# Moving the weight slots of a TensorE-bound layer: pitch 4160 bytes instead of 4096

## The chip, the cores and the metric

The kernel runs on one core of one Trainium2 chip. The metric is the time of one execution in device microseconds; the median of several executions counts, and lower is better.

## What is computed

One layer of a language model on 512 rows of 1024 numbers, all in float32: a gated feed-forward block (SwiGLU), a mixer of dilated attention and an mLSTM, an attention over 256 memory rows, and a second SwiGLU, each followed by a residual and a layer norm. Nearly all of the arithmetic is products of activations with weight matrices:

```python
def reference(x, mem, rel_bias, ln_g, ln_b, ffn_w_gate, ffn_w_up, ffn_w_down, w_in, ...):
    for l in range(DEPTH):          # DEPTH = 1
        x = layer_norm(ALPHA * x + 0.5 * swiglu(x, ffn_w_gate[l, 0], ffn_w_up[l, 0], ffn_w_down[l, 0]), ...)
        x = layer_norm(ALPHA * x + hybrid_mixer(x, w_in[l], ..., w_out[l], rel_bias), ...)
        x = layer_norm(ALPHA * x + memory_attention(x, mem, xq_w[l], xkv_w[l], xo_w[l]), ...)
        x = layer_norm(ALPHA * x + 0.5 * swiglu(x, ffn_w_gate[l, 1], ffn_w_up[l, 1], ffn_w_down[l, 1]), ...)
    return x
...
def swiglu(x, w_gate, w_up, w_down):
    return (jax.nn.silu(x @ w_gate) * (x @ w_up)) @ w_down
```

Here d_model is 1024, the feed-forward width 2816 (22 tiles of 128), and the mixer's input projection is 3592 wide.

## The kernel before

**Weights come in units.** All weights are cut into 204 units of 128 partitions by 1024 float32, 512 KB each, in the order in which they are used. SyncE's queue brings a unit into one of three `raw` tiles. ScalarE copies it, rounded to the type float32r, into `whi`; VectorE writes the rest, `raw - whi`, into `wlo` (line 1234 of the profile, in the helper `split`). There are six slots of each, `whi0` to `whi5` and `wlo0` to `wlo5`, and unit u lies in slot u mod 6. Activations are split in the same way: `xth`/`xtl` for the transposed input of a stage, `hhi`/`hlo` (six slots) for what a down projection reads, `mth`/`mtl` for the memory.

**Three matmuls make a product.** The helper `three` writes lines 393 to 395 of the profile: high by high, high by low, low by high, all into the same PSUM bank. With 128 by 128 stationary and 128 by 512 moving, these are the bulk of the program: 4,440 matmuls of 512 columns, and 384 more of the same kind with 256 columns. In a name like `ps<-xth,whi` the first is the moving operand and the second the stationary one, which a weight load (PEld) brings into the array ahead of its matmul.

- In `cols_part` (feed-forward up, projections) the stationary operand is a 128-column piece of a weight slot, and the activations move.
- In `product` (all four down or output projections), in `rows_block` and in the memory's value projection the weight slot's halves of 512 columns move, and pieces of the activations (`hhi`, `xth`, `mth`) are stationary.

**Order.** Every engine has a program of its own that is written out by hand, with loops over six units in the feed-forward stages; semaphores tie them together. A slot is used for a visit of 3, 6, 12 or 24 matmuls in a row before TensorE goes to another slot: counted over the program with its loops there are 380 visits, 128 of them of 3 matmuls, 80 of 6, 16 of 12 and 156 of 24.

**Addresses.** SBUF tiles are placed by a cursor. `sb()` gives the next bytes of every partition. In bytes within a partition, the kernel before has `whi0` at 32896 and every further slot 4096 on, `wlo0` at 57472, `raw0` at 82048, `hhi0` at 108416 and `xth` at 132992. The activations' pieces that a matmul uses start at multiples of 512 bytes from their tile's start, and so do those of a slot. Hence all 128-column weight pieces and all activation pieces have one fixed distance modulo 512 bytes: (32896 - 132992) mod 512 = 256. One small product is an exception: the gate projection, 24 matmuls of 512 columns with a stationary operand of only 36 columns, reads `wg_hi` at 225216 and `wg_lo` at 226368 with a step of 144 bytes from one k to the next.

Of the kernel before, what the change touches and what calls it, by code (L numbers as in the profile page):

```python
# [7 lines left out]
F32R = mybir.dt.float32r  # L8
# [4 lines left out]
P = 128  # L13
# [4 lines left out]
SPL = 6  # L18
# [37 lines left out]
def macaron_layer(nc, x, mem_cols, ln_g, ln_b, units, gate_cols, ig_bias, fg_bias, ml_g,  # L56
                  bias_by_key, lnm, conv_cols, g_rows, out):
    S, D = x.shape[1], x.shape[2]
# [52 lines left out]
    with ctx:  # L111

        KB = 1024
# [3 lines left out]
        cursor = [start]  # L117

        def at(name, shape, offset, dt=F32):
            return nc.alloc_sbuf_tensor_at(name, shape, dt, offset=offset)  # L120

        def sb(name, shape, dt=F32):
            n = 4
            for s in shape[1:]:
                n *= s
            t = at(name, shape, cursor[0], dt)
            cursor[0] += -(-n // 32) * 32
            assert cursor[0] <= start + size, "SBUF is full"
            return t

        xn = sb("xn", [P, NB, D])
        whi = [sb(f"whi{s}", [P, D], F32R) for s in range(SPL)]
        wlo = [sb(f"wlo{s}", [P, D], F32R) for s in range(SPL)]
        raw = [sb(f"raw{s}", [P, D]) for s in range(RAW)]
        ident = sb("ident", [P, P])
        mlg = sb("mlg", [P, MW])
# [1583 lines left out]
```

## Time and profile before

| | |
|---|---|
| time, median of 3 (lowest to highest) | 1194.47 us (1193.79 to 1195.27) |
| time of the profiled execution | 1195.15 us |
| its span in the profile | 1193.3 us |
| TensorE matmuls busy | 1181.4 us, 99% of the span |
| weight loads busy (beside the matmuls) | 968.0 us, 81% |
| VectorE busy | 539.5 us, 45% |
| ScalarE busy | 407.8 us, 34% |
| granted TensorE clock, mean | 0.995 of full speed |

The span is from the first to the last instruction; 1.85 us of the execution lie around it. A busy share near 100% says that some matmul was always under way, and not how fast they follow each other: matmuls overlap, and each lasts longer than the distance to the next one's start. The distances between starts are what sets the time here, and they are read from the timeline.

### The profile page before, as it was taken

To read this page: it belongs to the slowest core of one execution; us is meant where nothing else is said; L and a number is where in the kernel's file an instruction comes from. 1 tells how busy PE (TensorE), PEld (TensorE's weight loads), DVE (VectorE), ACT (ScalarE), POOL (GpSimd) and SP (SyncE) were. 2 spreads that over 40 slices of the span, in tenths; PEclk is the share of its full clock that TensorE was granted. 3 is DMA by queue.
4 is the path that set the end of the run, shared out by engine and by line. 5 is a ranking of instruction groups with operands and counts; after the bars stand their busy time and mean duration, and the time that the engine had idled before them with its cause. 6 is when DMAs were issued, how large, how long until landed. Compare 5 with 4: busy or idle time off the path is not lost.

```text
span 1193.3 us, 14742 instructions
## 1 busy us (share of the span) xinstructions
PE 1181.4 (99%) x5522; PEld 968.0 (81%) x5522; DVE 539.5 (45%) x840; ACT 407.8 (34%) x666; POOL 30.3 (3%) x45
## 2 busy tenths in 40 slices
PE   9999999999999999999999999999999999999997
PEld 8888888888888777788798887778988888888886
DVE  4533333443346544644885843337433333343335
ACT  5321222242324344433454454434322212232322
POOL 2000000000001011000000000000000000000000
PEclk9999999999999999999989999999999999999999
DMA  8523222232222221141333261122322232232311
GB/s 293 200 94 105 88 93 101 89 124 95 99 70 89 82 69 53 56 156 63 94 136 96 99 211 53 54 78 96 127 89 95 99 104 89 90 120 97 99 35 70
DMA packets 33563, 120.85 MB, mean 101 GB/s; under 512 B 3900, under 2 KB 3916, under 8 KB 33264
## 3 DMA queue, kind: packets, MB, share of 16 engines
q1 hardware_dynamic: 30528, 109.07, 27.5%
q0 software_dynamic: 2992, 11.19, 2.6%
q8 instruction: 30, 0.49, 0.2%
q14 instruction: 13, 0.11, 0.0%
HBM read 118.13 MB, written 2.11 MB: 101 GB/s over the span
## 4 chain that ended last, share of the span: by engine, by line
PE 99%; ACT 1%; DVE 0%; issue 0%; DVEq 0%; POOL 0%; POOLq 0%; ACTq 0%
PE ps L393 30%; PE ps L395 29%; PE ps L394 29%; PE ps L592 2%; PE ps L615 2%; PE ps L815 1%; PE ps L805 1%; PE ps L693 1%; PE ps L410 1%; PE ps L602 1%; PE ps L677 1%; PE ps L544 0%; PE ps L630 0%; PE ps L787 0%; ACT ew L844 0%
## 5 line engine op out<-in xcount | busy, mean ns | idle before, releaser
L1234 DVE TENSOR_TENSOR wlo<-raw,whi 128x1024 fp32r<-128x1024 f32 x196 | 240.5, 1231 | 413.2 <-ACT whi L844 412.3
L393 PE MATMUL ps<-xth,whi 128*128 128x512 f32 (+1 forms) x924 | 359.1, 389 | 0.0
L395 PE MATMUL ps<-xth,wlo 128*128 128x512 f32 (+1 forms) x924 | 353.2, 382 | 0.0
L394 PE MATMUL ps<-xtl,whi 128*128 128x512 f32 (+1 forms) x924 | 352.9, 382 | 0.0
L844 ACT ACTIVATE whi<-raw 128x1024 fp32r<-128x1024 f32 (+1 forms) x204 | 206.9, 1037 | 153.8 <-PE ps L395 141.8
L393 PEld LDWEIGHTS ps<-xth,whi 128*128 128x128 f32 x924 | 173.8, 188 | 34.1 <-issue 1.3
L394 PEld LDWEIGHTS ps<-xtl,whi 128*128 128x128 f32 x924 | 173.9, 188 | 33.8 <-issue 1.0
L395 PEld LDWEIGHTS ps<-xth,wlo 128*128 128x128 f32 x924 | 173.7, 188 | 33.6
L393 PE MATMUL ps<-whi,hhi 128*128 128x512 f32 x480 | 189.4, 395 | 0.0
L395 PE MATMUL ps<-whi,hlo 128*128 128x512 f32 x480 | 186.9, 389 | 0.0
L394 PE MATMUL ps<-wlo,hhi 128*128 128x512 f32 x480 | 186.8, 389 | 0.0
L844 ACT ACTIVATE eg<-ps 128x512 f32<-128x512 f32 x44 | 26.3, 598 | 326.3 <-PE ps L395 326.3
L393 PEld LDWEIGHTS ps<-whi,hhi 128*128 128x128 f32 x480 | 90.1, 188 | 19.3 <-issue 0.7
L395 PEld LDWEIGHTS ps<-whi,hlo 128*128 128x128 f32 x480 | 90.1, 188 | 19.0
L394 PEld LDWEIGHTS ps<-wlo,hhi 128*128 128x128 f32 x480 | 90.1, 188 | 18.8 <-issue 0.7
L1301 DVE SCALAR_TENSOR_TENSOR h<-eg,ps 128x512 f32 (+1 forms) x44 | 30.3, 688 | 82.2 <-PE ps L395 82.0
L844 ACT ACTIVATE squares<-xn,nmean 128x1024 f32<-128x1024 f32 x16 | 18.5, 1153 | 76.2 <-DVE nmean L1264 76.2
L393 PE MATMUL ps<-whi,xth 128*128 128x512 f32 x96 | 38.0, 396 | 0.0
L395 PE MATMUL ps<-whi,xtl 128*128 128x512 f32 x96 | 37.5, 390 | 0.0
L394 PE MATMUL ps<-wlo,xth 128*128 128x512 f32 x96 | 37.4, 389 | 0.0
L1261 DVE SCALAR_TENSOR_TENSOR xn<-xn,ps 128x512 f32<-128x512 f32 x32 | 21.3, 683 | 26.2 <-PE ps L395 26.2
L844 ACT ACTIVATE lg<-lg,nmax 128x128 f32<-128x128 f32 (+3 forms) x32 | 18.0, 562 | 42.7 <-DVE nmax L1406 42.7
(156 smaller groups left out, 936.0 us busy)
## 6 DMA issues: line engine op xcount, KB each, us to landing
raw<-in_units SPq DMA_DIRECT2D x204, 512.0 KB, 3.3
gb<-in_ln_g POOLq DMA_DIRECT2D x4, 512.0 KB, 3.8
gb<-in_ln_b POOLq DMA_DIRECT2D x4, 512.0 KB, 5.1
xn<-in_x POOLq DMA_DIRECT2D x4, 512.0 KB, 12.7
wb<-in_bias_by_key POOLq DMA_DIRECT2D x8, 256.0 KB, 3.7
out<-xn SPq DMA_DIRECT2D x8, 256.0 KB, 2.1
gsp<-g_rows POOLq DMA_DIRECT2D x1, 1024.0 KB, 7.3
memn<-in_mem_cols POOLq DMA_DIRECT2D x1, 1024.0 KB, 4.9
```

Source lines behind the costliest of these rows:

```text
L393: mm(dst, lh, rh, start=start, stop=False)
L394: mm(dst, lh, rl, start=False, stop=False)
L395: return mm(dst, ll, rh, start=False, stop=stop)
L410: last = nc.tensor.transpose(ps[2 * b + k // 4][:, (k % 4) * P:(k % 4 + 1) * P], xn[:, b, k * P:(k + 1) * P], ident[:, :])
L592: mm(ps[n % 2][:, 0:(i + 1) * P], qk[(2 * p) % 4][rows, i * P:(i + 1) * P], qk[(2 * p + 1) % 4][rows, 0:(i + 1) * P], start=True, stop=Tru ...
L602: last = nc.tensor.transpose(ps[2 + n % 2][:, j * P:(j + 1) * P], lg[n % 3][:, j * P:(j + 1) * P], ident[:, :])
L615: last = mm(ps[4 + n % 2][:, 0:HD], pt[n % PTS][:, j * P:(j + 1) * P], va[:, j, h * HD:(h + 1) * HD], start=j == 0, stop=j == i)
L677: mm(ps[j % 2][:, 0:S - j * P], qk[(2 * h + 1) % 4][:, j * P:(j + 1) * P], qk[(2 * h) % 4][:, j * P:S], start=True, stop=True).then_inc(kq ...
L844: return nc.scalar.activation(*a, **k)
L1234: v.tensor_tensor(wlo[c % SPL][:, :], raw[c % RAW][:, :], whi[c % SPL][:, :].bitcast(F32), ALU.subtract).then_inc(lo_done, 1)
L1261: step.inc(v.scalar_tensor_tensor(out=half, in0=half, scalar=ALPHA, in1=ps[2 * b + h][:, :], op0=ALU.mult, op1=ALU.add, accum_out=xsum[:, ...
L1301: v.scalar_tensor_tensor(out=dst, in0=e[:, :], scalar=0.25, in1=ps[bank + 1][:, :], op0=ALU.mult, op1=ALU.mult).then_inc(h_done, 1)
```

## The change

The cursor no longer gives the slots one after another. They are put at addresses of their own, 4160 bytes apart (4096 + 64). The first `whi` slot lies 256 bytes behind the cursor, and the `wlo` slots 25088 bytes behind the `whi` slot of the same number, a multiple of 512. Everything that is allocated later moves up by 1152 bytes.

```diff
         xn = sb("xn", [P, NB, D])
-        whi = [sb(f"whi{s}", [P, D], F32R) for s in range(SPL)]
-        wlo = [sb(f"wlo{s}", [P, D], F32R) for s in range(SPL)]
+        PITCH = 4 * KB + 64
+        slots = [cursor[0] + 256, cursor[0] + 256 + SPL * PITCH + 128]
+        whi = [at(f"whi{s}", [P, D], slots[0] + s * PITCH, F32R) for s in range(SPL)]
+        wlo = [at(f"wlo{s}", [P, D], slots[1] + s * PITCH, F32R) for s in range(SPL)]
+        cursor[0] = slots[1] + SPL * PITCH
         raw = [sb(f"raw{s}", [P, D]) for s in range(RAW)]
```

`whi0` is now at 33152, `whi1` at 37312, and so on; `wlo0` at 58240, `hhi0` at 109568, `xth` at 134144. The distance between slot s and the activations, modulo 512, was 256 for every slot; it is now 384 + 64 s, so 384, 448, 0, 64, 128 and 192 for slots 0 to 5. Slots 1, 3 and 5 are at 64 modulo 128 from the activations, slots 0, 2 and 4 at 0. No instruction is added, removed or moved on any engine or queue, no operand changes its size or type, and no semaphore or wait changes; behind the edit the line numbers are 3 higher.

## Rows read from the trace of the kernel before

**Rows 1.** The page: span, engines' busy time, chain that ended last.

```profile
span 1193.3 us, 14742 instructions
PE 1181.4 (99%) x5522; PEld 968.0 (81%) x5522; DVE 539.5 (45%) x840; ACT 407.8 (34%) x666; POOL 30.3 (3%) x45
...
PE 99%; ACT 1%; DVE 0%; issue 0%; DVEq 0%; POOL 0%; POOLq 0%; ACTq 0%
```

**Rows 2.** Waits: engine line waited for, total us, times, longest us.

```profile
DVE wlo L1234 <- ACT whi L844: 412.3, 113, 12.5
...
ACT whi L844 <- PE ps L395: 141.8, 46, 3.9
...
PEld ps L615 <- ACT pt L844: 9.1, 14, 0.8
...
PE ps L693 <- DVE pt L1480: 1.6, 1, 1.6
```

**Rows 3.** Timeline of TensorE: start us, duration us; three moments 100 us apart.

```profile
99.92 0.39 PE L393 MATMUL ps<-xth,whi 128*128 128x512 f32 x1
...
199.88 0.39 PE L393 MATMUL ps<-xth,whi 128*128 128x512 f32 x1
...
299.84 0.39 PE L393 MATMUL ps<-whi,hhi 128*128 128x512 f32 x1
```

**Rows 4.** Stretches, line 394 alone: length, busy (matmuls), clock, DMA, GB/s.

```profile
50.00:350.00 300.00, 171.67 (x442) 1.00 0.29 96
850.00:1180.00 330.00, 188.87 (x486) 1.00 0.27 91
```

**Rows 5.** Timeline, matmuls of 256 columns.

```profile
836.01 0.28 PE L393 MATMUL ps<-xth,whi 128*128 128x256 f32 x1
...
836.37 0.28 PE L393 MATMUL ps<-xth,whi 128*128 128x256 f32 x1
```

**Rows 6.** Timeline, plain float32 matmuls of 512 columns, and their group.

```profile
761.82 1.88 PE L815 MATMUL ps<-xpt,vmem 128*128 128x512 f32 x4
...
L815 PE MATMUL ps<-xpt,vmem 128*128 128x512 f32 x32 | 14.9, 592 | 0.0
```

**Rows 7.** Timeline into, through and out of the gate projection.

```profile
389.16 0.39 PE L393 MATMUL ps<-whi,xth 128*128 128x512 f32 x1
...
389.84 0.39 PE L393 MATMUL ps<-xth,wg_hi 128*36 128x512 f32 x1
390.07 0.39 PE L394 MATMUL ps<-xtl,wg_hi 128*36 128x512 f32 x1
390.30 0.39 PE L395 MATMUL ps<-xth,wg_lo 128*36 128x512 f32 x1
390.52 0.39 PE L393 MATMUL ps<-xth,wg_hi 128*36 128x512 f32 x1
...
392.61 0.39 PE L393 MATMUL ps<-xth,wg_hi 128*36 128x512 f32 x1
392.84 0.39 PE L394 MATMUL ps<-xtl,wg_hi 128*36 128x512 f32 x1
393.06 0.40 PE L395 MATMUL ps<-xth,wg_lo 128*36 128x512 f32 x1
...
395.38 0.40 PE L393 MATMUL ps<-xth,whi 128*128 128x512 f32 x1
```

**Rows 8.** Timeline after transposes have broken the stream.

```profile
361.01 0.39 PE L394 MATMUL ps<-wlo,hhi 128*128 128x512 f32 x1
...
361.71 0.39 PE L394 MATMUL ps<-wlo,hhi 128*128 128x512 f32 x1
361.93 0.39 PE L395 MATMUL ps<-whi,hlo 128*128 128x512 f32 x1
362.16 0.40 PE L393 MATMUL ps<-whi,hhi 128*128 128x512 f32 x1
362.40 0.39 PE L394 MATMUL ps<-wlo,hhi 128*128 128x512 f32 x1
...
363.09 0.39 PE L394 MATMUL ps<-wlo,hhi 128*128 128x512 f32 x1
```

**Rows 9.** VectorE's splits: duration ns min/median/max, first and last start.

```profile
L1234 DVE TENSOR_TENSOR wlo<-raw,whi x196: 1192/1225/2712, 22.5 to 1154.9; 128x1024 fp32r<-128x1024 f32 x196
```

## The prediction

> **What bounds the kernel now.** I read the page first. TensorE is busy for 99% of the span and makes up 99% of the chain that ended last [rows 1]. The list of waits says the same from the other side: TensorE's longest wait for another engine is 1.6 us in one matmul, and its weight loads wait for ScalarE for 9.1 us in all, inside the attention; VectorE on the other hand waits 412.3 us for ScalarE's halves of the splits, and ScalarE 141.8 us for TensorE to give slots back [rows 2]. So only a change in the distance between matmul starts can move the time much.
>
> That distance is astonishingly constant. Three starts of line 393 lie 99.96 and again 99.96 us apart [rows 3]. Line 394 has 442 matmuls in the 300 us from 50 to 350 [rows 4], so about 147 per 100 us, and with the other two lines 441 matmuls: 99.96 / 441 = 226.7 ns each. The third of these starts lies in the down projection, where the weight slot moves and `hhi` is stationary, while in the first two it is the other way round. So through every slot, through the change of role, and through all multiples of 512 bytes within the tiles, the distance stays the same. The stretch 850 to 1180 has 486 in 330 us, the same pace [rows 4]. The granted clock is 1.00 there, which is the 2.4 GHz level: 512 columns are 213.3 ns, and 13.3 ns come on top. With 256 columns three matmuls take 0.36 us [rows 5], so 120 ns each, 106.7 + 13.3: the same addition. The plain float32 matmuls don't have it: four of them last 1.88 us from first start to last end, one lasts 592 ns, so three distances are 1.29 us and one 429 ns, against 426.7 ns for 1024 array cycles [rows 6], so some 2 ns on top. The 4,440 matmuls of 512 columns are 4,440 x 226.7 ns = 1006.5 us, 84% of the span, and 11 ns in each, 49 us, are this unexplained addition. The question of the change is whether that addition depends on the distance between the addresses of the two operands.
>
> **What the change costs, part by part.** The addresses are the only thing that changes, and there are four places where they could act.
>
> (a) *The steady pace in slots 0, 2 and 4.* Their distance to the activations was 256 modulo 512 and is now 384, 0 and 128. Between 199.88 and 299.84 the moving address goes from `xth` (384 modulo 512) to `whi` (128), a move by 256, with no mark in the 226.7 ns [rows 3]. Nothing before shows a move by 128. I take 0 for these.
>
> (b) *The steady pace in slots 1, 3 and 5*, now at 64 modulo 128. The nearest rows are those of the gate projection. At its k = 0, `wg_hi` lies 64 bytes from `xth` modulo 512 (225216 - 132992) and `wg_lo` 192, both a position that the odd slots get. The matmuls start at 389.16, 389.84 and 390.52: three distances before and three after the entry are 0.68 us each, so 226.7 ns, while the stationary operand changed from distance 256 to 64 and to 192 [rows 7]. At k = 4 the distances are 128 and 256: 392.61, 392.84, 393.06 is 0.45 us for two, again the old pace [rows 7]. The same projection also shows the other bound. Its steps of 144 bytes put most k at 16, 32 or 48 modulo 64, and from 390.52 to 395.38 its 21 matmuls take 4.86 us, 231.4 ns each, 4.7 ns more [rows 7]. So positions do matter when they are off a multiple of 64. All slots are at multiples of 64 before and after. The low bound for 2,220 matmuls in the odd slots is 0, the high one 2,220 x 4.7 ns = 10.4 us. I take 0, by the rows with the same positions.
>
> (c) *The jump by 64 bytes from visit to visit.* When the stream is disturbed, it doesn't return to 226.7 ns at once: after transposes, nine distances from 361.01 to 363.09 are 2.08 us against 9 x 226.7 = 2.04, so 41 ns over [rows 8]. They alternate: 361.71 to 361.93 is 0.22, 362.16 to 362.40 is 0.24 [rows 8]. If each of the 380 visits began such a walk, its cost would be 41 ns in the 172 visits of 12 or 24 matmuls, and by the same walk, cut off at six and at three matmuls, some 29 ns in 80 visits and 18 ns in 128: 7.1 + 2.3 + 2.3 = 11.7 us. The entry to the gate projection, a jump by 192 bytes, began none [rows 7]. That gives 0 at the low end. I take 1 ns a visit, 0.4 us.
>
> (d) *The other engines.* VectorE reads `raw` and `whi` together, until now at equal positions modulo 4096, and takes 1225 ns [rows 9]; that may become somewhat less or more. It is covered: a unit lasts 24 x 226.7 ns = 5.4 us on TensorE, a split 1.2 us, and VectorE waits 412.3 us in all [rows 2]. Even 300 ns more in each of 196 splits would be 59 us in those waits. If that cover went, in the attention, what is late next is the weight load that waits for `pt`, now 9.1 us in all [rows 2]; I put it at 0. Transfers, their sizes and targets in number are the same.
>
> Sum: 0 + 0 + 0.4 + 0 us. The profiled execution took 1195.15 us (span 1193.3), 0.7 us over the median of 1194.47; I put the sum on the median: 1194.9 us.
>
> The Trainium skill, page "TensorE: Matmul & The Clock Gate", section "Part 2: What happens when you issue a matmul", says that TensorE has two independent SBUF read ports, one for the moving operand and one for weight loads, so that a load takes no bandwidth from the running matmul. By that rule no distance of addresses could matter, in either direction, and the change would be worth 0. The same section gives N / 2.4 + 2.5 ns for the distance of warm matmuls, which is 215.8 ns; the float32 rows agree with the 2.5, and the float32r rows at 226.7 do not. So the rule's arithmetic leaves 11 ns that something takes, and the gate projection shows that positions can add to them.
>
> **The rivals.**
>
> *Faster: the 11 ns are a conflict of the two read streams.* Weight load and moving stream start nearly together in every matmul, all at one distance modulo 512. If that distance is a bad one, and other multiples of 64 are better, up to 11 ns a matmul come back: at most 49 us, 1146 us. More likely only some slots gain, or all gain little: the shortest distance that the walk shows is 0.22 us [rows 8]; I take its upper end, 224 ns, 2.7 ns less, which over all 4,440 is 12 us, 1182.5 us. For it speaks that the addition exists at all, that float32 matmuls, which take their moving columns at half the rate, don't have it, and that the walk shows shorter distances. Against it: a stationary operand of 36 columns (28% of the load) paid the full addition in three matmuls, at two other distances [rows 7], and 256 columns pay as much as 512 [rows 5]. A conflict would shrink with the load. Chance 0.21.
>
> *Slower: positions at 64 modulo 128 never settle.* The mechanism is that of the gate projection's later k, 231.4 ns instead of 226.7. It would come in the odd slots, or where these move, for which there is no row at all: the moving address has never been at an odd multiple of 64 from its usual one. In the odd slots alone it gives 10.4 us, 1205 us; in all slots 20.9 us, 1215 us. It decides from 0.54 ns a matmul on, 2.4 us in all. For it: those rows. Against it: k = 0 and k = 4. Chance 0.16.
>
> *Slower: a walk at each visit*, as in (c): between 0.4 and 11.7 us, with the middle near 6, 1200 us. For it speaks the length of the walks after a break; against it the entry at 389.84 and the way from stationary `whi` to stationary `hhi` between 199.88 and 299.84, neither of which begins one. Chance 0.10.
>
> *No change*, since positions in steps of 64 bytes don't count: chance 0.53, 1193 to 1197 us by itself.
>
> **How the numbers follow.** A measurement of this kernel tells about 0.2%, 2.4 us, from no change. The walk at small cost ends within that in a third of its cases, as would the smallest of the other two: faster 0.21, same 0.55, slower 0.24. The range goes down to 1183 us, which takes in a gain of up to 2.6 ns a matmul and leaves out the larger ones, and up to 1205 us, which takes in the walks and the unsettled odd slots and leaves out unsettled slots everywhere; that leaves some 0.2 outside. The likeliest case gives 1194.9.
>
> **What the changed profile would show.** If I am right, three starts of line 396 (393 before) stay 99.96 us apart, through slots of both kinds, and busy time and matmul counts per stretch don't move. If slots differ, the distance within a unit of 24 matmuls changes with a period of six units, about 33 us, and the timeline of two neighbouring units shows it: 5.44 us for each now. A walk shows as the first 4 to 9 distances of a unit between 224 and 236 ns and the rest at 226.7. A gain by (a) shows as 215 to 224 ns in every unit. VectorE's median of 1225 ns will tell whether its two reads at equal positions cost anything; it should leave the end where it is. What would make the prediction wrong is above all the moving operand at 64 modulo 128, in 1,824 matmuls of which half are in odd slots, since no row covers it.

## The result, and the profile after

The changed kernel takes 1210.5 us (median of 4, 1210.18 to 1211.34), the kernel before 1194.82 us (median of 4): the ratio is 1.0136, with a 95% interval of 1.0124 to 1.0147. It is slower by 15.7 us, and 5.5 us beyond the upper end of the predicted range.

The page of the changed kernel, span, busy times and VectorE's splits:

```profile
span 1208.7 us, 14742 instructions
...
PE 1196.9 (99%) x5522; PEld 966.8 (80%) x5522; DVE 537.5 (44%) x840; ACT 407.6 (34%) x666; POOL 31.3 (3%) x45
...
L1237 DVE TENSOR_TENSOR wlo<-raw,whi 128x1024 fp32r<-128x1024 f32 x196 | 239.5, 1226 | 423.0 <-ACT whi L847 422.4
```

Against [rows 1] the span grew by 15.4 us and TensorE's busy time by 15.5, while VectorE and ScalarE are no busier. The number of instructions is the same. VectorE's wait for ScalarE grew from 412.3 to 422.4 us, and ScalarE's for TensorE to give slots back from 141.8 to 146.3. So nobody keeps TensorE waiting; its matmuls follow each other more slowly.

Two stretches, one inside the first up projections and one inside the first down projection; columns as in [rows 4], but all matmuls counted. First the kernel before:

```profile
60.00:240.00 180.00, 180.00 (x795) 1.00 0.29 95
256.00:346.00 90.00, 90.00 (x399) 1.00 0.28 94
```

and the changed kernel:

```profile
60.00:240.00 180.00, 180.00 (x783) 1.00 0.29 96
256.00:346.00 90.00, 90.00 (x391) 1.00 0.30 98
```

The counts include some 1.7 matmuls that began before the stretch, so the paces are about 180 / 793.3 = 226.9 ns and 180 / 781.3 = 230.4 ns, and for the down projection 90 / 397.3 = 226.5 and 90 / 389.3 = 231.2; they are good to 0.3 ns, and where a pace below differs from such a quotient, the unrounded starts decide. The granted clock is 1.00 in all four. The loss is spread over the whole stretch, and the timeline shows how. These are the starts of seven units of 24 matmuls, in slots 1, 2, 3, 4, 5, 0 and 1, and then four starts in the down projection, of slots 0, 1, 2 and 3:

```profile
56.20 0.40 PE L396 MATMUL ps<-xth,whi 128*128 128x512 f32 x1
...
61.70 0.40 PE L396 MATMUL ps<-xth,whi 128*128 128x512 f32 x1
...
67.16 0.40 PE L396 MATMUL ps<-xth,whi 128*128 128x512 f32 x1
...
72.76 0.39 PE L396 MATMUL ps<-xth,whi 128*128 128x512 f32 x1
...
78.33 0.39 PE L396 MATMUL ps<-xth,whi 128*128 128x512 f32 x1
...
83.84 0.39 PE L396 MATMUL ps<-xth,whi 128*128 128x512 f32 x1
...
89.41 0.40 PE L396 MATMUL ps<-xth,whi 128*128 128x512 f32 x1
...
283.26 0.39 PE L396 MATMUL ps<-whi,hhi 128*128 128x512 f32 x1
...
288.83 0.39 PE L396 MATMUL ps<-whi,hhi 128*128 128x512 f32 x1
...
294.42 0.39 PE L396 MATMUL ps<-whi,hhi 128*128 128x512 f32 x1
...
299.90 0.40 PE L396 MATMUL ps<-whi,hhi 128*128 128x512 f32 x1
```

The units take 5.50, 5.46, 5.60, 5.57, 5.51 and 5.57 us, where each took 5.44. Divided by 24 and read from the unrounded starts, with the stationary operand's distance from the moving one (stationary minus moving address, modulo 256 bytes; why 256 and not 512 is shown below the table and by the pairs):

| | slot 0 | 1 | 2 | 3 | 4 | 5 |
|---|---|---|---|---|---|---|
| up: distance | 128 | 192 | 0 | 64 | 128 | 192 |
| up: ns a matmul | 232.2 | 229.3 | 227.5 | 233.2 | 232.3 | 229.4 |
| down: distance | 128 | 64 | 0 | 192 | 128 | 64 |
| down: ns a matmul | 232.1 | 232.8 | 228.4 | 229.6 | 232.8 | 233.5 |

Away from the first and last units of each projection these values repeat from round to round within 0.1 ns. Slots 0 and 4 lie 256 bytes apart in their distance modulo 512 (384 and 128), and so do slots 1 and 5 (448 and 192); each pair has one pace. In the down projection the weight slot moves and `hhi` is stationary, so the sign of its distance turns, and slots 1 and 5 change places with slot 3. Only slot 2, at distance 0 modulo 256, has the later starts of each unit 226 and 227 ns apart. In the up projection its first four are 236, 228, 233 and 231, a walk of some 20 ns in all; in the down projection the first ten (228, 229, 234, 236, 224, 231, 235, 229, 232, 231) are some 42 ns over. These walks are what its means show.

Where the 15.4 us of span lie, read from the two timelines: the stream starts again after transposes at 360.70 us in the kernel before and at 368.31 in the changed one, 7.6 us later; the second feed-forward block's 512-column stream starts at 848.97 and at 858.03, so 9.1 us later; and the end is 15.4 us later. The two feed-forward parts lost 7.6 and 6.3 us, and the 490 us between them only 1.5. Two parts of these differences are not the change's. Of the 7.6 us 0.8 are the very first matmuls, of which three follow each other at 427 or 594 ns in the changed kernel and none at more than 335 ns in the kernel before. And in the memory attention, where TensorE has idled for 1.34 and 1.60 us, the granted clock of the kernel before fell to the 1.2 GHz level (0.50) and that of the changed kernel did not (1.00). The same 20 matmuls of 129 columns, and the distance to what follows, took 4.3 us before and 2.3 after. A row of the timeline and a stretch inside it (columns as above), first before, then changed:

```profile
599.37 4.67 PE L693 MATMUL ps<-vx,pt 128*128 128x129 f32 x20 [1.60 <-DVE pt L1480]
...
599.40:603.60 4.20, 4.20 (x19) 0.50 0.00 0
```

```profile
609.24 2.50 PE L696 MATMUL ps<-vx,pt 128*128 128x129 f32 x20 [1.60 <-DVE pt L1483]
...
609.30:611.40 2.10, 2.10 (x19) 1.00 0.00 0
```

With the first matmuls behind them these distances hide 2.4 us of the change's cost. The clock's fall does not follow the addresses: of the kernels below that ran at the old pace, the one with weights and activations moved together kept the clock at 1.00 there (profiled execution 1193.57 us), and the one with pairs of slots lost it for a part of this stretch (1194.6 us). So without the clock the 490 us lost 3.9 and not 1.5.

### The profile page after: what moved, and what is told of

The parts are those of the page before. It is cut to its first block, busy times and chain, and to the rows that moved or that the text cites. A ratio compares the mean times of both kernels' runs of the same rounds, so it can differ in the third digit from the quotient of the medians.

```text
span 1208.7 us, 14742 instructions
## 1 busy us (share of the span) xinstructions
PE 1196.9 (99%) x5522; PEld 966.8 (80%) x5522; DVE 537.5 (44%) x840; ACT 407.6 (34%) x666; POOL 31.3 (3%) x45
## 4 chain that ended last, share of the span: by engine, by line
PE 99%; ACT 1%; DVE 0%; issue 0%; DVEq 0%; POOL 0%; POOLq 0%; ACTq 0%
PE ps L396 30%; PE ps L398 29%; PE ps L397 29%; PE ps L595 2%; PE ps L618 2%; PE ps L818 1%; PE ps L808 1%; PE ps L413 1%; PE ps L696 1%; PE ps L605 1%; PE ps L680 1%; PE ps L547 0%; PE ps L633 0%; PE ps L790 0%; ACT ew L847 0%; PE ps L434 0%
## 5 line engine op out<-in xcount | busy, mean ns | idle before, releaser
L1237 DVE TENSOR_TENSOR wlo<-raw,whi 128x1024 fp32r<-128x1024 f32 x196 | 239.5, 1226 | 423.0 <-ACT whi L847 422.4
L847 ACT ACTIVATE whi<-raw 128x1024 fp32r<-128x1024 f32 (+1 forms) x204 | 206.7, 1036 | 158.1 <-PE ps L398 146.3
L847 ACT ACTIVATE squares<-xn,nmean 128x1024 f32<-128x1024 f32 x16 | 18.5, 1153 | 78.5 <-DVE nmean L1267 78.5
```

Of the source, the lines that this page charges most:

```text
L847: return nc.scalar.activation(*a, **k)
L1237: v.tensor_tensor(wlo[c % SPL][:, :], raw[c % RAW][:, :], whi[c % SPL][:, :].bitcast(F32), ALU.subtract).then_inc(lo_done, 1)
```

## The experiments

**Theory A**: the pace of float32r matmuls depends on the distance between stationary and moving operand modulo 256 bytes, and 0 is the cheapest. **Theory B**: what costs is the jump from slot to slot, a walk at each visit. **Theory C**: the position of the slot itself counts. The kernels below place each slot at its address in the kernel before plus an offset in bytes, given for the high and the low slots; `room` is by how much everything behind the slots moves up. Up to the gate projection's, the kernels differ from the kernel before in lines like these.

**All slots moved by 64 bytes** (pitch 4096, no jumps):

```diff
-        whi = [sb(f"whi{s}", [P, D], F32R) for s in range(SPL)]
-        wlo = [sb(f"wlo{s}", [P, D], F32R) for s in range(SPL)]
+        hi_off, lo_off, room = [64] * 6, [64] * 6, 512
+        whi = [at(f"whi{s}", [P, D], cursor[0] + s * 4 * KB + hi_off[s], F32R) for s in range(SPL)]
+        wlo = [at(f"wlo{s}", [P, D], cursor[0] + (SPL + s) * 4 * KB + lo_off[s], F32R) for s in range(SPL)]
+        cursor[0] += 2 * SPL * 4 * KB + room
```

> All twelve weight slots moved by the same 64 bytes against the activations, pitch 4096 as before. Theory A (each matmul's pace depends on the distance stationary minus moving operand modulo 256): where the weight slot is stationary the distance is 64 modulo 256, so 233.4 ns a matmul in every unit; where it moves the distance is 192, so 229.1 ns; together about 2,592 x 6.7 + 1,824 x 2.4 = 22 us more, somewhat less since the mixed stages are disturbed already before: 1209 to 1217 us. Theory B (a jump between slots at each visit starts a walk): no slot jumps here, so 226.7 ns everywhere and 1194 to 1196 us.

Measured: 1212.82 us, ratio 1.0152 (1.0135 to 1.0169). The same two stretches:

```profile
60.00:240.00 180.00, 180.00 (x773) 1.00 0.27 94
256.00:346.00 90.00, 90.00 (x395) 1.00 0.30 104
```

180 / 771.3 = 233.4 ns with stationary weights and 90 / 393.3 = 228.8 with moving ones. Every unit of every slot has the same mean, 233.33 and 228.9. Without one jump the kernel is 18.2 us slower, and theory B falls as the account of the loss.

**Slots in pairs, 256 bytes apart** (offsets 0, 0, 256, 256, 512, 512 for the high and 512, 512, 768, 768, 1024, 1024 for the low slots, room 1024):

> Slots 2 and 3 lie 256 bytes further from the activations than slots 0 and 1, slots 4 and 5 512 bytes: every second visit changes the position, by 256 bytes, and no distance changes modulo 256. Theory A: 226.7 ns everywhere, 1193 to 1197 us. Theory B: a walk at each jump, 3 to 8 us more. A theory with a period of 512 bytes (distance 0 instead of 256 is bad): slots 2 and 3 slower.

Measured: 1194.81 us, ratio 1.0001 (0.9991 to 1.0011).

```profile
60.00:240.00 180.00, 180.00 (x796) 1.00 0.28 95
256.00:346.00 90.00, 90.00 (x399) 1.00 0.28 94
```

226.7 ns in all units. A jump of 256 bytes costs nothing here, and distances 0 and 256 modulo 512 have one pace; with the slot pairs 0 and 4, 1 and 5 above, the pace has the period 256.

**Weights and activations moved together by 64 bytes** (offsets 64, room 64):

> Slots and all that is allocated behind them, the activations too, moved up by 64 bytes together: absolute addresses change, distances between weights and activations don't. Theory A: 226.7 ns everywhere, 1193 to 1197 us. Theory C (the address of the slot itself counts, not its distance to the other operand): a slower pace as in e1, 1209 to 1217 us.

Measured: 1194.62 us, ratio 1.0001 (0.9991 to 1.001).

```profile
60.00:240.00 180.00, 180.00 (x796) 1.00 0.28 96
256.00:346.00 90.00, 90.00 (x399) 1.00 0.28 97
```

The slots lie where the first experiment had them, at the old pace. Theory C falls; the distance counts.

**All slots moved by 192 bytes** (room 512):

> The mirror of the shift by 64: all slots moved by 192 bytes, pitch 4096. Theory A with the sign (the distance is stationary minus moving, modulo 256, so that 64 and 192 swap with the roles): 228.9 ns where the weight slot is stationary, 233.3 where it moves. The shift by 64 cost 18.2 us where full streams would give 2,592 x 6.67 + 1,824 x 2.2 = 21.3, so 0.85 of it; here 2,592 x 2.2 + 1,824 x 6.67 = 17.9, times 0.85 is 15.2 us: 1208 to 1212 us. A theory in which only the size of the distance counts (64 away in either direction is the same) gives the same pace in both roles and the 1213 us of the shift by 64.

Measured: 1211.14 us, ratio 1.014 (1.0123 to 1.0157), within the range that theory A gave.

```profile
60.00:240.00 180.00, 180.00 (x788) 1.00 0.28 96
256.00:346.00 90.00, 90.00 (x387) 1.00 0.28 94
```

180 / 786.3 = 228.9 and 90 / 385.3 = 233.6 (233.3 from the unrounded starts): the roles have changed places, so the distance has a sign.

**Offsets in steps of 32 bytes, one slot each** (0, 32, ..., 160; low slots 256 higher):

> Slots 0 to 5 at distances 0, 32, 64, 96, 128 and 160 modulo 256 where the weight slot is stationary, and at 0, 224, 192, 160, 128 and 96 where it moves. Theory A: slot 0 at 226.7, slot 2 at 233.4 as stationary and 229.1 as moving, slot 4 at 232.5 in both; slots 1, 3 and 5 are new, and 160 and 96 must show the same pace in both roles. Time some 1205 to 1213 us. If only jumps counted, all six slots would have the same mean.

Measured: one run, 1218.65 us, above what was expected. Up, slots 0 to 5: 228.6, 233.0, 233.4, 233.7, 233.4, 233.3 ns; down: 226.8, 233.5, 229.4, 233.8, 233.3, 234.1. Slot 2 came as expected. So did slot 0 down; up it pays a walk of some 40 ns in its first eight distances and then stands at 226.7. Distance 160 shows means of 233.3 as stationary and 233.8 as moving weights, 96 shows 233.7 and 234.1, but these differences are walks: behind the first eight or so starts both roles run through the same cycles (231, 232 and 237 at 160; seven values from 231 to 238 at 96). Slot 4, at 128, does have another pace than in the changed kernel: 238 and 229 in turn, 233.4 instead of 232.3, and the same down. So at that distance two paces are possible, and theory A in its simple form is incomplete.

**The same, 16 bytes off** (16, 48, ..., 176; the offsets of the run before, with the contents of each slot starting four elements further on):

> Slots 0 to 5 at distances 16, 48, 80, 112, 144 and 176 modulo 256 as stationary, 240, 208, 176, 144, 112 and 80 as moving operand, high and low parts congruent. Theory A in its simple form (only distance 0 is clean, everything else pays 2 to 7 ns): each slot between 228.9 and 235 ns, each constant from round to round, 1210 to 1222 us. If there is a distance better than 0, this run or the one in steps of 32 finds it as a slot below 226.7 ns. Distances 80, 112, 144 and 176 stand in both roles and must show the same pace in both.

Measured: one run, 1216.61 us, within what was expected. Up: 233.4, 233.2, 231.7, 233.3, 233.2, 230.5; down: 231.8, 233.2, 231.2, 231.1, 233.2, 231.0. None is below 226.7. Distance 112 agrees in both roles (233.3 as stationary, 233.2 as moving weights), 80 and 176 nearly do (231.7 and 231.0; 230.5 and 231.2), and 144 does not (233.2 and 231.1): again more than one pace at one distance.

**Low slots at another distance than high ones** (high 0, low 128, room 512):

> High slots where they were (distance 0 modulo 256), low slots at 128: what undoing the congruence of high and low parts does. Theory A: of the three matmuls of a product one has its distance at 128 (5.6 to 6.7 ns more), and if each change of distance disturbs the stream as well, all three are above 226.7: mean between 228.6 and 234 ns in every slot, 1201 to 1220 us. If changes of distance between matmuls cost nothing beyond the matmul concerned, the mean is 228.6 to 228.9.

Measured: one run, 1208.47 us; 231.1 ns up, 228.9 down, the same in each slot. Up, the distances between starts go 227, 232, 234, 227, 232, 235, so more than the one matmul in three is hit; down they go 227, 234, 226, and one is. Keeping high and low parts at one distance modulo 256 is worth having.

**The gate projection at distance 64** (its k step 256 bytes instead of 144, the weight slots as before):

```diff
-        wg_hi = at("wg_hi", [P, KT, GW], ..., F32R)
-        wg_lo = at("wg_lo", [P, KT, GW], ... + KT * GW * 4, F32R)
+        wg_hi = at("wg_hi", [P, KT, 64], ..., F32R)
+        wg_lo = at("wg_lo", [P, KT, 64], ... + KT * 64 * 4, F32R)
...
```

The lines left out write and read the first 36 columns of each step.

> Only the gate projection's two stationary tiles get a pitch of 256 bytes from one k to the next instead of 144, so that all of its 24 loads of 36 columns lie at 64 modulo 256 from the moving operand. Theory A1 (distance alone counts, the load's length doesn't): 233.3 ns each after the first few, so 5.58 us from its first start to the next product's. Theory A2 (a load of 36 columns meets the moving stream less long, so pays less): between 226.7 and 229 ns, 5.44 to 5.50 us. The kernel's time stays within 1193 to 1197 us by both.

Measured: one run, 1193.1 us. The first start of the projection and the first after it:

```profile
390.71 0.39 PE L393 MATMUL ps<-xth,wg_hi 128*36 128x512 f32 x1
...
396.15 0.39 PE L393 MATMUL ps<-xth,whi 128*128 128x512 f32 x1
```

24 matmuls in 5.44 us, 226.7 each, where 128 columns at this distance pay 233.3. This is the row on which the prediction stood, and it is no accident of three matmuls: in this projection, with its 36 columns, distance 64 costs nothing. That distance alone counts (A1) is refuted.

**Load lengths.** Four extra series of 24 matmuls ahead of the gate projection, in three kernels whose slots are moved by 64, 128 and 192 bytes:

```diff
+            need(U_QK)
+            for cols in (32, 64, 96, 128):
+                for k in range(KT):
+                    c = slice(k * P, k * P + cols)
+                    three(ps[1][0:cols, :], whi[U_QK % SPL][:, c], wlo[U_QK % SPL][:, c],
+                          xh[:, k, :], xl[:, k, :], k == 0, k == KT - 1)
             pe.wait_ge(wg_done, 1)
```

> The shift of all slots by 64 bytes, and four extra series of 24 matmuls (8 products of three, 512 columns) ahead of the gate projection, which read 32, 64, 96 and 128 columns of a weight slot as stationary operand at distance 64. They write a PSUM bank that is overwritten afterwards. Theory D (what is paid grows with the length of the weight load): 32 columns 226.7 ns, as the 36 of the gate projection, 128 columns 233.3, 64 and 96 between or with a step. Theory E (the gate projection was free at 64 only because it was entered from a settled stream, and the state is kept): all four series 233.3 or unsettled, since the stream is at 233.3 or 229 ahead of them. Kernel's time 1213 + 96 x 0.23 = 1235 us by both.

> The same series with all slots moved by 128 bytes. Theory D: 32 columns near 226.7 ns, 128 columns 232.3 or 233.4 (the two paces that distance 128 has shown). The down stages, with no jump between slots and distance 128 in both roles, show which of the two paces stays without one. If every full stream is at 232.3 to 233.4: before + 0.85 x 4,416 x 5.6 to 6.7 ns = 21 to 25 us, plus 22 us for the series: 1237 to 1242 us.

> The same series with all slots moved by 192 bytes. Theory D: 226.7 ns for 32 columns, 228.9 for 128. If the point at which a longer load begins to cost differs between distances 64, 128 and 192, the load and the moving stream meet at a place that depends on the distance; if it is the same length in all three, it is the length alone. Kernel's time 1211 + 22 = 1233 us.

Measured, one run each: 1236.27, 1238.27 and 1230.82 us, and per matmul over each series of 24, from the unrounded starts, for 32, 64, 96 and 128 columns: at distance 64 231.6, 232.6, 228.3 and 233.4 ns; at 128 230.4, 231.2, 231.9 and 232.2; at 192 231.9, 228.7, 233.4 and 229.3. The first runs a little over and the last under what was expected of the whole kernel. The cost does not grow with the load, and 32 columns at distance 64 pay 5 ns where 36 had paid none. Theory D falls.

**Does the entry decide?** The slots as before, and twelve series added, four widths at each of the distances 64, 192 and 128; each series of 21 at a nonzero distance follows 12 settling matmuls at distance 0, the distance made by starting the slices 16, 48 or 32 elements later.

> All slots as before the change. Ahead of the gate projection, twelve pairs of series in the slot of the next unit: 12 settling matmuls (128 columns at distance 0) and then 21 matmuls with a stationary operand that starts 64, 192 or 128 bytes further on and has 32, 64, 96 or 128 columns. Theory D fell for unsettled entries (32 columns at 64 paid 231.7 ns); here each series is entered from a settled stream. Theory E (the settled state survives a bad distance as long as the load is short): 32 columns at 64 stay at 226.7 ns, as the gate projection's 36 did, and 128 columns at 64 leave for 233.3. If 32 columns at 64 leave 226.7 here too, the gate projection was free for another reason than its entry. All widths at 233.3, 228.9 and about 232.5 would mean that neither length nor entry counts.

Measured: the first row is the first start of 32 columns at 64, the second the next start behind it; then the same for 96 columns at distance 128.

```profile
393.56 0.40 PE L395 MATMUL ps<-xth,whi 128*32 128x512 f32 x1
...
398.41 0.39 PE L395 MATMUL ps<-xth,whi 128*128 128x512 f32 x1
...
469.31 0.39 PE L395 MATMUL ps<-xth,whi 128*96 128x512 f32 x1
...
474.07 0.39 PE L395 MATMUL ps<-xth,whi 128*128 128x512 f32 x1
```

4.85 us for 21 matmuls is 231.0 ns: also from a settled stream, 32 columns at 64 leave 226.7. So theory E does not explain the gate projection. But the second pair is 4.76 us, 226.7 ns, for 96 columns at 128, which from an unsettled stream took 231.9. So the entry seems to matter at some distances (the two runs also make the distance in different ways, by the slot and by the slice), and the width matters, in no simple order. What sets the gate projection's free matmuls apart is not shown: besides its width its k step is 256 bytes where the series have 512, and no run has 32 or 128 columns at its step.

**A map of all distances from a settled stream**, 128 columns stationary, 512 and 256 columns moving:

> Slots as before the change. Ahead of the gate projection, for each distance from 16 to 240 bytes in steps of 16: 12 settling matmuls of 512 columns at distance 0, 21 of 512 columns at that distance, 12 settling ones and 21 of 256 columns, all with 128-column stationary operands. From the runs so far: 512 columns at 64, 128 and 192 at 233.3, 232.3 and 228.9 ns, and no distance below 226.7; 256 columns at 113.5 or 117.8 at 64 and at 117.8 at 192, against 120 at 0. A distance below 226.7 ns for 512 columns would be a better place for all slots, and would refute that 0 is the best.

Measured: ns a matmul, mean of 18 distances in each series, from the unrounded starts.

| distance | 16 | 32 | 48 | 64 | 80 | 96 | 112 | 128 | 144 | 160 | 176 | 192 | 208 | 224 | 240 |
|---|---|---|---|---|---|---|---|---|---|---|---|---|---|---|---|
| 512 columns | 226.7 | 233.3 | 233.3 | 233.3 | 232.0 | 234.4 | 233.2 | 231.9 | 226.7 | 233.3 | 230.3 | 228.9 | 231.8 | 233.3 | 226.7 |
| 256 columns | 118.5 | 118.2 | 117.8 | 117.8 | 118.6 | 117.2 | 119.8 | 118.9 | 118.3 | 120.0 | 118.1 | 113.3 | 116.9 | 116.7 | 120.0 |

In the timeline, 21 matmuls of 512 columns at 144 between the first two rows, and then six of 256 columns at 192:

```profile
485.89 0.39 PE L395 MATMUL ps<-xth,whi 128*128 128x512 f32 x1
...
490.65 0.28 PE L395 MATMUL ps<-xth,whi 128*128 128x256 f32 x1
...
527.69 0.28 PE L395 MATMUL ps<-xth,whi 128*128 128x256 f32 x1
...
528.37 0.28 PE L395 MATMUL ps<-xth,whi 128*128 128x256 f32 x1
```

4.76 / 21 = 226.7 and 0.68 / 6 = 113.3 ns. With 512 columns no distance has a pace below 226.7. Distances 16, 144 and 240 hold it when they are entered from it; the slots at 16 and 144 in the run 16 bytes off, entered from their neighbours, ran at 233.4 and 233.2. Every settling series at distance 0 came back to 226.7 within nine matmuls. With 256 columns the order is another: 0 is, with 160 and 240, the slowest place, and 192 the fastest.

**Only the memory's tiles moved**, by 192 bytes and with them the keys and what is laid behind them, so that the key projection's 256-column matmuls have distance 64, and the slots stay:

```diff
-        mth = at("mth", [P, KT, MB * P], ar + 32 * KB, F32R)
-        mtl = at("mtl", [P, KT, MB * P], ar + 40 * KB, F32R)
+        mth = at("mth", [P, KT, MB * P], ar + 32 * KB + 192, F32R)
+        mtl = at("mtl", [P, KT, MB * P], ar + 40 * KB + 192, F32R)
...
```

> Weight slots as before the change; the memory's tiles, keys and what is laid behind them move up by 192 bytes, so that the key projection's 192 matmuls of 256 columns have distance 64 instead of 0, and the memory's value projection, 96 matmuls of 512 columns with moving weights, distance 192. From the shift by 64: 256 columns at 113.5 ns instead of 120 (or 117.8, its other pace), so 192 x 6.5 = 1.2 us less, at least 0.4; 512 columns at 228.9 instead of 226.7, so 0.2 us more. Sum -0.2 to -1.0 us: 1193.6 to 1194.4 beside 1194.6. If 256-column matmuls were faster there for another reason than the distance, no change or +0.2 us.

Measured: 1193.57 us (median of 11) beside 1194.4 (median of 15), ratio 0.9991 (0.9982 to 1.0). Two starts of the key projection, 24 matmuls apart:

```profile
622.17 0.28 PE L393 MATMUL ps<-mth,whi 128*128 128x256 f32 x1
...
624.89 0.28 PE L393 MATMUL ps<-mth,whi 128*128 128x256 f32 x1
```

2.72 / 24 = 113.3 ns against 120 in [rows 5]. The trace shows the gain where it was expected. In the time it is 0.8 us, of the size of the sum, and the interval just reaches no change; executions of one kernel differ by as much with the clock.

## Why the prediction was wrong

**What bounds the kernel** was right: only the distance between matmul starts moved the time, by 15.5 us of TensorE's busy time in a span longer by 15.4.

**(a), slots 0, 2 and 4**, is the step that took the time out of the range. It was "Nothing before shows a move by 128. I take 0 for these", without an upper bound. Distance 128 costs 5.6 ns a matmul (232.3 instead of 226.7). Slot 2, the only one at 0 modulo 256, did settle at the old pace. By the slot means above, the three slots cost 9.2 us. The row that stood for the move by 256, the crossing at 299.84 in [rows 3], did not bear on the distance at all: there the stationary operand changes from `whi` to `hhi` as the moving one changes from `xth` to `whi`, and the distance stays 256 modulo 512. That 256 is free only the pairs showed. For 128 there was one row, k = 4 of the gate projection, which the prediction reads under (b): a load of 36 columns at the old pace.

**(b), slots 1, 3 and 5**, failed in its point. "I take 0, by the rows with the same positions" rested on loads of 36 columns. Distance 64 costs 6.6 ns, above the 4.7 ns of the upper bound, and 192 costs 2.7, inside it; together the three slots cost 10.0 us, just within the bound of 10.4. So (a) and (b) weigh about the same, and the range had room for one of them alone. The gate projection with its distance fixed at 64 shows that the reading of [rows 7] was correct and its carrying over was not: 36 columns are free there, 32 columns in a weight slot pay 4.3 ns, 128 pay 6.7. The rows of k = 0 were evidence for a form of instruction that the change does not touch.

**(c), the jump between visits**: the walk exists where the new distance is another modulo 256. Slot 2's units in the changed kernel show some 20 ns up and some 42 ns down, so the upper bound of 41 was about right and the 1 ns taken was not. It is seen by itself only at distance 0, and is counted in the slot means above. Where the distance stays the same modulo 256 a jump is free (the pairs). In slot 2 it comes to some 0.9 us, an estimate from 2,592 / 144 = 18 units at 20 ns and 1,824 / 144 = 12.7 units at 42 ns.

**(d), the other engines**: right. VectorE's two reads no longer start at equal positions, and the median split still takes 1225 ns; the waits grew and covered everything.

**The size.** With the measured means of the six slots, 2,592 matmuls with stationary weights times 4.0 ns and 1,824 with moving ones times 4.9 ns give 19.3 us. Measured were 15.7, and 15.4 in the two profiled spans. Set side by side start by start, the 512-column matmuls took 18.5 us more; the mixed stages gave less than their slots' means, since their streams are broken so often that they stood at 227 to 249 ns already before. The 384 matmuls of 256 columns took 47.6 us before and 46.2 after, 1.4 less. The clock in the memory attention took off 2.4 more, which is luck of these two executions, and everything else added 0.7.

**The rivals.** The conflict by address was described with the wrong sign and then given the weight of a gain: with 512 columns the 13.3 ns above the array's 213.3 at distance 0 are the least that any distance showed, and other distances add to it. With 256 columns, where the prediction read the same addition as a reason against a conflict, it did shrink with the distance, from 13.3 to 6.6 ns above 106.7. The slower rival named the right thing (no return to 226.7 in the odd slots, 1205 us) and its wider form (all slots, 1215 us) was nearest to the result; it was limited to odd slots because (a) had been settled at 0. The rule of the Trainium skill, "TensorE: Matmul & The Clock Gate", section "Part 2", that the two read ports are independent, would make all distances equal. The runs at 64 and 192 bytes do not agree with that for float32r with 512 moving columns, by up to 6.7 ns a matmul, and the measurement decides.

## What stays open

Why the distance matters is not shown. That both streams read at once, and that one gives way to the other where their positions meet, fits the sign and the period of 256 bytes, and in the trace of the kernel before a weight load of 0.19 us starts within 0.01 us of the matmul ahead of its own; against a simple form of it stand the widths, where 32, 36, 64 and 96 columns are neither free nor costly in order. What makes a stream keep one of two paces is not shown either. Nor is shown where the 13.3 ns at distance 0 come from; no run without a weight load in the stream was made.

## What to carry to other kernels

Where TensorE is the bound and its operands are float32r, keep the stationary and the moving operand of every matmul at one distance modulo 256 bytes, 0 for 512 columns, through all slots and both roles; a pitch that is a multiple of 256 does it, and high and low parts should have the same distance. With 256 moving columns 0 was not the best. A row speaks for an instruction only if its form is the same, the number of columns of the weight load included; if the nearest row has another form, its value is not a point but an end of the range, and a place with no row at all gets a bound too. An address experiment with a different distance in each slot is a cheap measurement, since the timeline then gives one pace for each.

## What was not expected of the hardware

- The pace of a stream of 512-column float32r matmuls settles at 226.67 ns at distance 0, and at other distances in cycles of starts that repeat: 236 and 231 in turn at 64, 226, 229 and 232 at 192, and seven values between 228 and 241 at 128.
- Some distances have two stable paces, and which one a stream takes seems to depend on how it enters: 96 columns at 128 ran at 226.7 or 231.9, 128 columns at 144 at 226.7 or 233.2, and at 128 at 232.3 or 233.4.
- Matmuls of 256 columns go the other way: 120.0 ns at distance 0, and 113.3 to 117.8 at 64 and 192.
- In the same place of the program, after idle times of 1.34 and 1.60 us, the granted clock fell to 0.50 in some executions (the kernel before) and stayed at 1.00 in others (the changed kernel); that was worth 2.4 us.
- ScalarE's and VectorE's splits did not notice the positions: 1037 and 1231 ns in the mean before, 1036 and 1226 after.
